# Encoder layer: the first gate/up unit pair by plain products, the gate applied on reading the banks, the last three down pairs by tile

## What is computed

```python
def _swiglu(u, w_gate, w_up, w_down):
    return (jax.nn.silu(u @ w_gate) * (u @ w_up)) @ w_down
...
        def sublayer(h, j, fn, resid_w):
            shift = mods[:, 3 * j][:, None]
            scale = mods[:, 3 * j + 1][:, None]
            gate = mods[:, 3 * j + 2][:, None]
            u = (_layer_norm(h) * (1.0 + scale) + shift).astype(h.dtype)
            z = DEEPNORM_ALPHA * h.astype(jnp.float32) + resid_w * gate * fn(u)
            return (_layer_norm(z) * ln_g[layer, j] + ln_b[layer, j]).astype(h.dtype)

        h = sublayer(h, 0, lambda u: _swiglu(u, ffn1_w_gate[layer], ffn1_w_up[layer], ffn1_w_down[layer]), 0.5)
        h = sublayer(h, 1, lambda u: _mixer(u, w_in[layer], rpb[layer], w_out[layer]), 1.0)
        h = sublayer(h, 2, lambda u: _swiglu(u, ffn2_w_gate[layer], ffn2_w_up[layer], ffn2_w_down[layer]), 0.5)
```

## Time and profile before

| | us |
|---|---|
| median of 3 runs | 2321.95 (2320.61 to 2324.6) |
| the profiled execution | 2320.21 |
| its span | 2318.4 |
| PE busy | 2044.4 (88% of the span) |
| DVE, ACT, POOL busy | 1172.1, 768.6, 764.3 |
| first FFN, from its first transfer to its last DVE instruction | 51.60 to 834.14 |
| second FFN, likewise, then to the end | 1561.88 to 2314.41, 2318.4 |

### The profile page before, as it was taken

One profiled execution on the slowest core, in us unless ns is written; L12 is line 12 of the kernel. 1 busy time (PEld: TensorE's weight loads), 2 busy tenths in 40 slices (PEclk: granted clock), 3 DMA queues, 4 the chain that ended last, 5 costly groups with the idle time before them and its releaser, 6 DMA issues. The chain is left out here.

```text
span 2318.4 us, 27274 instructions
## 1 busy us (share of the span) xinstructions
PE 2044.4 (88%) x10302; PEld 1585.8 (68%) x10302; DVE 1172.1 (51%) x1859; ACT 768.6 (33%) x1273; POOL 764.3 (33%) x450
## 2 busy tenths in 40 slices
PE   3599999999799929999988889874899999979996
PEld 2477777777688826766666666653788888868885
DVE  4854454554457483344324443568643434426655
ACT  3533323332223143344323333226433333322231
POOL 0632222222866530000032210234422222248592
PEclk8799999999899969999999999986999999989998
DMA  7144444444443221101142111602222222355432
GB/s 261 54 153 148 127 150 147 133 148 171 177 157 135 82 82 64 55 11 44 55 87 61 19 36 37 227 9 100 73 87 78 87 77 91 109 200 175 152 111 98
DMA packets 157128, 247.33 MB, mean 107 GB/s; under 512 B 7873, under 2 KB 106449, under 8 KB 156881
## 3 DMA queue, kind: packets, MB, share of 16 engines
q1 hardware_dynamic: 125890, 211.36, 26.7%
q10 hardware_dynamic: 30096, 30.25, 4.3%
q0 software_dynamic: 1024, 4.13, 1.2%
HBM read 205.09 MB, written 40.63 MB: 106 GB/s over the span
## 5 line engine op out<-in xcount | busy, mean ns | idle before, releaser
L1263 PE MATMUL f_ps<-f_uh,f_ops 128*128 128x512 f32 x2464 | 787.9, 397 | 56.6 <-DVE f_ops L1070 51.7
L1263 PEld LDWEIGHTS f_ps<-f_uh,f_ops 128*128 128x128 f32 x2464 | 466.2, 189 | 185.3 <-DVE f_ops L1070 54.0
L1263 PE MATMUL f_ps<-f_ul,f_ops 128*128 128x512 f32 x1232 | 485.9, 394 | 0.0
L862 POOL TENSOR_TENSOR f_wd<-f_wd,f_gates 128x1024 f32<-128x1024 f32 x88 | 259.0, 2967 | 153.4 <-DMA f_wd<-in_ffn_w_down 153.0
L1309 PE MATMUL f_ps<-f_wdh,f_hdh 128*128 128x512 f32 x704 | 277.1, 394 | 25.7 <-DVE f_hdl L1154 23.7
L1309 PE MATMUL f_ps<-f_wdl,f_hdh 128*128 128x512 f32 x704 | 276.2, 392 | 0.0
L1309 PE MATMUL f_ps<-f_wdh,f_hdl 128*128 128x512 f32 x704 | 275.9, 392 | 0.0
L853 POOL TENSOR_TENSOR f_sums<-f_raw 128x512 f32<-128x512 f32 x88 | 117.8, 1339 | 474.4 <-DVE f_ops L1070 327.3
L1263 PEld LDWEIGHTS f_ps<-f_ul,f_ops 128*128 128x128 f32 x1232 | 233.4, 189 | 47.7
L1151 DVE TENSOR_TENSOR f_wdl<-f_wd,f_wdh 128x2048 fp32r<-128x2048 f32 x44 | 117.8, 2678 | 217.9 <-ACT f_wdh L1000 217.9
L1070 DVE TENSOR_TENSOR f_ops<-f_sums,f_ops 128x512 fp32r<-128x512 f32 x176 | 133.6, 764 | 162.2 <-ACT f_ops L915 162.1
(11 more groups left out here) (209 smaller groups left out, 2731.7 us busy)
## 6 DMA issues: line engine op xcount, KB each, us to landing
f_wd<-in_ffn_w_down SPq DMA_DIRECT2D x44, 1024.0 KB, 4.9
f_raw<-in_ffn_w_gate SPq DMA_DIRECT2D x22, 1024.0 KB, 5.6
f_raw<-in_ffn_w_up SPq DMA_DIRECT2D x22, 1024.0 KB, 5.7
f_hidden<-acc SPq DMA_DIRECT2D x88, 256.0 KB, 2.2
f_hd<-f_hidden SPq DMA_DIRECT2D x44, 512.0 KB, 4.1
f_aw<-in_w_ada ACTq DMA_DIRECT2D x28, 512.0 KB, 3.5
acc<-in_w_ada ACTq DMA_DIRECT2D x28, 512.0 KB, 3.5
in_raw<-in_w_in SPq DMA_DIRECT2D x24, 512.0 KB, 6.7
```

Of the source, the lines that this page charges most:

```text
L862: ins = nc.gpsimd.tensor_tensor(mem.wd[:, n % 2, c, :], mem.wd[:, n % 2, c, :], mem.gates[:, :], ALU.mult)
L1263: done = nc.tensor.matmul(ps[:, bank, :], l[:, k, :], r[:, u, k, :], start=fresh and k == 0 and m == 0, stop=closed and k == HK - 1 and m ...
```

## The change

**Gate and up.** Units 0 and 1 are done by 16 plain products (8 each), first half of the tokens before the second (`plain_product`); units 2 to 21 by seven as before, so 156 products. The plain products need no `T` sum: their operands are `B11`, `B21`, `B22` and the fourth token block (its high part lies in the place of `T4`, its low part in that of `T2` until the sums come). `T1` to `T4` are made, split and used from unit 2 on. In the second FFN the normalisation of tiles 4 to 7 moves behind the first half's modulation.

```diff
+PLAIN = 16
+SPARE = PLAIN - RING
+LAST = 3
...
-    seq = [(0, 1), (0, 2), (1, 1), (1, 2)]
-    for j in range(NU_F):
...
+    seq = [(2, 1)]
+    for j in range(2, NU_F):
+        seq += [(j, 2), (j, 5), (j, 6), (j, 3), (j, 7)]
+        if j + 1 < NU_F:
             seq.append((j + 1, 1))
         seq.append((j, 4))
...
+        def plain(p):
+
+            return p // 8, p // 4 % 2, p // 2 % 2, p % 2
...
+            def plain_product(p):
+
+                half, kk, j, f = plain(p)
+                o = p % 8
+                pe.wait_ge(w_lo, o + 1)
+                if half == 0:
+                    pe.wait_ge(lo0, HK * (kk + 1))
+                    high, low = ((B11, B11), (B21, B21))[kk]
+                else:
+                    pe.wait_ge(mod_done[0], KT)
+                    pe.wait_ge(mod_done[1], KT)
+                    pe.wait_ge(lo_b if kk else lo_a, HK)
+                    high, low = ((T4, T2), (B22, B22))[kk]
+                multiply(PLAIN_BANK[half][j][f], o, uh[:, high], ul[:, low], kk == 0, kk == 1)
...
             for y in range(KT):
                 turn(y)
-            for y in range(KT, 2 * KT):
-                turn(y)
-                if y % 2:
-                    product(*seq[(y - KT) // 2])
+            for p in range(PLAIN):
+                plain_product(p)
+                if p in (1, 2):
+                    for y in range(4):
+                        turn(KT + 4 * (p - 1) + y)
```

**Down.** POOL no longer touches `w_down` or `h`. The gate, halved once, multiplies each bank when it is read, and the scaled `h` is added in the same instruction that multiplies it by alpha:

```diff
-            def scale_down(n):
-                pool.wait_ge(wd_ld[n % 2], 16 * (n // 2 + 1))
-                for c in range(2):
-                    ins = nc.gpsimd.tensor_tensor(mem.wd[:, n % 2, c, :], mem.wd[:, n % 2, c, :], mem.gates[:, :],
-                                                  ALU.mult)
...
             def split_down(n):
-                act.wait_ge(wd_sc, n + 1)
+                act.wait_ge(wd_ld[n % 2], 16 * (n // 2 + 1))
...
+                    nc.vector.tensor_tensor(mem.ev[:, 2 * (t % 2) + i, :], ps[:, b, :], mem.gates[:, NB * i:NB * i + NB],
+                                            ALU.mult).then_inc(d_gated, 1)
+                dve.wait_ge(h_ld[t], 16)
...
+                    nc.vector.scalar_tensor_tensor(acc[:, t, cols], acc[:, t, cols], ALPHA, mem.ev[:, 2 * (t % 2) + i, :],
+                                                   ALU.mult, ALU.add).then_inc(d_out, 1)
...
+            for n in range(2 * PAIRS - LAST):
+                down(n, range(4))
+            for tiles in ((0, 1), (2,), (3,)):
+                for n in range(2 * PAIRS - LAST, 2 * PAIRS):
+                    down(n, tiles)
```

More of the change, by code:

```diff
@@ L284, in coefficients @@
         nc = self.nc
-        mean, var, std, y_, a_, b_, r, nb = (self.sm[:, 2 * g:2 * g + 2, i] for i in range(12, 20))
-        dve.wait_ge(self.std_done, 2 * g + 2)
+        first, last = self.groups[g][0], self.groups[g][-1]
+        mean, var, std, y_, a_, b_, r, nb = (self.sm[:, first:last + 1, i] for i in range(12, 20))
+        dve.wait_ge(self.std_done, last + 1)
         self.chained(dve, nc.vector.reciprocal(y_, std))
@@ new lines, in hi @@
+            def hi(o):
+                if o < RING:
+                    act.wait_ge(raw_ld[plain(o)[2]], 16)
+                else:
+                    j, i = seq[o - RING]
+                    if i in (1, 2, 4):
+                        act.wait_ge(raw_ld[j % 2], 16 * (j // 2 + 1))
+                    else:
+                        act.wait_ge(s_done, 4 * (j - 2) + (5, 6, 3, 7).index(i) + 1)
+                    act.wait_ge(mm, o + 1)
+                nc.scalar.copy(op(o)[0], source(o)).then_inc(w_hi, 1)
@@ new lines, in sum_hi, with plain_out @@
+            def sum_hi(u, k):
+                act.wait_ge(t_done, summed_at(u, k))
+                nc.scalar.copy(uh[:, u, k, :], t_sum(u, k)).then_inc(t_hi, 1)
+            def plain_out(p):
+                half, kk, j, f = plain(p)
+                if kk == 1 and j == 0:
+                    act.wait_ge(mm, p + 1)
+                    nc.scalar.activation(sil((0, 3, 1, 2)[2 * half + f]), ps[:, PLAIN_BANK[half][j][f], :], ACT.Silu
+                                         ).then_inc(silu_p, 1)
@@ L1111, in _ @@
                     low0(y - 2)
+                if y > HK:
+                    lo(y - HK - 1)
             low0(KT - 2)
+            lo(HK - 1)
             low0(KT - 1)
[L1114 to L1121 removed]
+            if ln is not None:
+                ln.coefficients(dve, 2)
+                ln.coefficients(dve, 3)
             if keep is not None:
@@ L1184, in _ @@
                 if n == PAIRS + 1:
-                    for b in range(8):
-                        add_down(0, b)
+                    dve.wait_ge(g_half, 1)
+                    for t in range(4):
+                        add_down(t)
                 if n == PAIRS + 2:
@@ L1291, in _, with bank_free, down @@
                     h += 1
-            def down(n):
+            def bank_free(b):
+                if b < 3:
+                    pe.wait_ge((c21_s, c11, c12)[b], (PAIRS - 1, NU_F - 3, NU_F - 3)[b])
+                elif b < 6:
+                    pe.wait_ge((pr, c11, c12)[b - 3], (4 * PAIRS, NU_F - 2, NU_F - 2)[b - 3])
+                else:
+                    if ada is not None:
+                        pe.wait_ge(a_row, ROUNDS)
+            def down(n, tiles):
                 pe.wait_ge(wd_lo, n + 1)
@@ L1312, in down @@
                                                     stop=p == PAIRS - 1 and c == 1 and m == 2)
-                    done.then_inc(d_mm, 1)
-            for n in range(2 * PAIRS):
-                down(n)
+                    if n < 2 * PAIRS - LAST or n == 2 * PAIRS - 1:
+                        done.then_inc(d_mm, 1)
+            for n in range(2 * PAIRS - LAST):
[3 more added lines that the diff above has]
+                    down(n, tiles)
 def band_start(t):
```

555 lines of the change are left out of this document (289 added, 266 removed).

## The result

The changed kernel takes 2240.55 us (median of 4 runs, 2236.88 to 2241.65) against 2321.4 (4 runs, 2320.61 to 2324.6): ratio 0.9649, with a 95% interval of 0.9638 to 0.9661, so 80.9 us less. Forecast were 2237 and a range of 2225 to 2256. The profiled execution has a span of 2239.6 us against 2318.4, 78.8 less, where the sum had 84.4.

A forecast was written before the change was run, and what follows sets the result against it. Time was taken to go at both FFNs' entries, waits in down and the tails, around long product stretches with PE busy. Terms summed to 84.4 us off the profiled 2320.21, 2235.8, forecast as 2237, range 2225 to 2256.

The forecast's parts named there:

- Down, handover: Start of down 1.9 us sooner in all; both down stretches fall to 239.7, saving 16.1 and 14.5.
- Leaving: End of each FFN: tile 7 out 13.0 us behind PE's end, saving 1.8 and 2.6.
- the lock: Tail: DVE instructions with two SBUF inputs and POOL's block each other; without it tile 7 out at +8.2, 5 us earlier.
- The step taken at 0.60: Tail: DVE's scalar_tensor_tensor on 128x512, not in the trace, taken at 0.60 us like a two-tensor instruction of this size.
- First product, first FFN: Entry: only the shorter list of high parts and low parts counts, so the first product comes 3.9 us earlier.
- First product, second FFN: Entry: half the normalisation and four high parts fewer ahead of it, so the first product begins 8.2 us earlier.
- The wait for the second half: Second FFN's entry: PE, after two plain products, waits 2.0 us for ACT's normalisation and the first modulated blocks.
- the slow start: PE beginning at the lower clock: first product's 12 matmuls take 5.27 us, not 2.735, costing 2.5.
- What feeds the second eight: Second half's plain products: DVE's four rounds last 16.4 us; plain product 7 waits at most 1 us.
- Rival 1: Second eight plain products starve on late DVE low parts: time 2250 to 2262; chance 0.16.
- The slack by (2,6): DVE's low parts, results and weight splits, some 31 us, done by 1642, when (2,6) needs T2: 2 us of slack.
- Rivals 2, 3 and 4: Clock falls at waits, 2262 to 2317 (0.06); steady products slip, 2335 (0.03); no lock, no second-half wait, 2225 (0.09).

The follow-up runs named there:

- e1: The kernel before with only the new down part and leaving, gate and up left as before: 2281.68 us, ratio 0.9828.
- e2: The changed kernel with all eight transfers of h issued ahead of the loads of pass 2, POOL still scaling nothing: 2251.44 us.
- e3: The changed kernel without POOL's multiplication by ln_g and addition of ln_b for tiles 4 and 5 (computation left out): 2229.93 us.
- e8: The changed kernel with both FFNs' entries laid out again, first weight split ahead of the first high part, transposes behind plain products 2 and 3: 2244.86 us.
- e4: The changed kernel with down's last three passes in the old order, all four tiles in each pass: 2260.61 us.
- e7: The changed kernel with tiles 4 and 5 apart too: last three passes tile by tile, own coefficients for each: 2239.74 us.
- e9: The changed kernel with down's first operands split one product earlier, and tiles 4 to 7 all finished tile by tile on DVE: 2230.25 us.
- e5: The changed kernel with the second half's transposes behind plain products 2 and 3 in place of 1 and 2: 2240.55 us.
- e10: The e9 kernel with only the second FFN's entry laid out again, normalisations earlier, transposes there behind plain products 2 and 3: 2223.27 us.

## Why the prediction was right

- **Down, handover.** 239.4 and 239.2 us against 239.7: right. e1 confirms that this half is worth what its terms say, and e2 that the order of the transfers was a cause by itself. Pass 2 was split 11.1 us after its load was issued (1987.13 to 1998.22), forecast 11.5. Two readings were off. POOL's scaling of `h` was named as part of pass 2's chain and wasn't in it; and e2 had the transfer at 12.2 us to ACT's start, not 17.3. How much POOL's share by itself was worth stays open.
- **Leaving.** Tile 6 out at +4.9, tile 7 at +12.9 (forecast +5 and +13.0), and e3 took the lock away for the 8.2. The step taken at 0.60 measured 0.64 to 0.71.
- **First product, first FFN.** This term failed: 8.6 us after the first transpose, against 10.85 before, 2.2 gained and not 3.9. The step "only the shorter list counts" left out the transfer. ACT's row in the kernel after:

```profile
59.39 0.62 ACT L906 CAST f_ops<-f_raw 128x512 fp32r<-128x512 f32 x1 [1.45 <-DMA f_raw<-in_ffn_w_gate]
```

  e8 shows the same transfer as a bound.
- **First product, second FFN.** 20.4 us after the stage's start; forecast 20.5.
- **The wait for the second half** was taken at 2.0 and measured 4.87. ACT sets the moment: the tiles were normalised 10.6 us behind the first product, where the sum had 9.3. The step that sized it had ACT going from the weight splits straight to the four tiles, but ACT first waited 1.63 us for coefficients that stand on DVE behind the last low parts:

```profile
1548.44 4.63 ACT L297 ACTIVATE f_nrm<-acc,f_in_sm 128x1024 f32<-128x1024 f32 x4 [1.63 <-DVE f_in_sm L292]
```

  The larger part of the difference is PE, which was there 2.2 us sooner than the sum had it, since its first two products ran at full clock (5.8 us, not 8.0). That gained nothing: in e2, e3, e4, e7 and e9 these two products took 7.4 to 7.5 us, the wait 3.1 to 3.3, and the transposes began after the same 10.6. So the sum charged the slow start where it was free, at the first product, and left it out behind the wait, where it counts: the 32 transposes took 5.0 us and not 3.2, and the product between them 3.3 and not 2.7. The 13 plain products behind took 0.233 us a matmul and not 0.228, 0.7 more in all. So (2,1) began 75.6 us after the stage's start, not 72.0.
- **What feeds the second eight.** The rounds took 15.1 us against 16.4, and plain product 7 had no wait. Rival 1 didn't come, though it was near: e5 takes one product of cover away, and PE waits 1.7 to 1.8. The slack by (2,6) was put at 2 us; in the kernel after the copy that needed `T4`'s last low part was done at 1602.84 for a product at 1605.9, so 3.1, and e10, in which PE came to (2,6) 7.7 us sooner after the first transpose and DVE to that low part only 3.0, ran out of it.
- **The rest.** The last product of the second FFN took 4.4 us in place of 2.9, a slow product behind a wait that is as old as the kernel.

Of what the profile after was to show, one line was wrong: PE does wait over 3 us between the first plain product and the last pass (4.87), though for the normalisation and not for a low part. (POOL also halves the gate once per FFN, 1.28 us.)

Together, by the stretches: gate and up with their entries gave 40.0 us where the sum had 47.5. In the first FFN 1.7 are missing at the first product and 1.3 behind it; in the second 3.6 at (2,1), and 1.0 behind it, where the slow last product stands. Handover and down gave 0.8 more than the sum, the tails what it had. So the edited parts missed it by 6.8. The spans missed it by 5.6 only because the mixing block took 1.7 less than in the kernel before and the conditioning rows 0.5 more, which is luck. What the change takes away was named rightly; the terms of the two entries were too large.

Rivals 2, 3 and 4: the clock did fall once, behind the wait of 4.87 us, and cost some 2 us, but neither stretch of plain products lies below a mean clock of 0.94; the steady products don't wait (idle 3.40 and 2.46 us, of which 2.45 and 2.46 stand before the last product, and 0.95 at a conditioning matmul); and 2225, which needed both no lock and no wait, was reached only by removing them.

## What to carry to other kernels

Price each part of a change on the stretch where its wait ends, and let one run with a part alone tell where a missing term lies. When PE is made to start earlier, ask of each input which is the last to come now, transfers too: a list of instructions that gets shorter helps only down to the landing of its data. Work that is moved off a full engine onto one that shares its port can land in the one place where nothing covers it; a tail of 8 us on one engine was better than the same tail shared between two.
